# A chunked recurrence on one core: the products and small inverses are made two tiles ahead, and U is solved by two 64-token blocks

## The chip, the core and the metric

The kernel runs on one core of a Trainium2 chip. The metric is the device time of one execution in microseconds (us). The core has five engines: TensorE (PE; its weight loads are shown apart as PEld), VectorE (DVE), ScalarE (ACT), GpSimd (POOL) and the queue that issues transfers (SP). All five run their own instruction streams and wait for each other on semaphores.

## The reference, cut to what matters

One layer of a hybrid encoder block over 1024 tokens and 1024 columns: a norm, one input projection, an RWKV-7 time-mixing group (8 heads of 64) beside windowed attention (8 heads), an output projection, and a SwiGLU feed-forward part. The change is in the recurrence of the RWKV group alone:

```python
def step(S, inp):
    r_t, w_t, k_t, v_t, kk_t, a_t = inp
    sa = jnp.einsum('bhvk,bhk->bhv', S, -kk_t)
    S = (S * w_t[:, :, None, :]
         + sa[..., None] * (kk_t * a_t)[:, :, None, :]
         + v_t[..., None] * k_t[:, :, None, :])
    return S, jnp.einsum('bhvk,bhk->bhv', S, r_t)
_, o = lax.scan(step, S0, xs)
```

The decay is w = exp(-0.6065 * sigmoid(...)), so products of decays over tokens are exponentials of cumulative sums.

## The kernel before

The scan is done in 8 tiles of 128 tokens, in float32. Within a tile the state update becomes a triangular system for each head: U = (I - N)^-1 R, where N (strictly triangular, 128x128) holds the products of alpha (the scaled kk) with beta (the scaled kk times a, the array `ab`), and R = alpha S + K V. Then the outputs are O = rho S + (masked k products) V + (masked beta products) U, and the new state is S + kt V + bt U. The names in the code:

- `cumulative` (L1130): the cumulative sums of the log decays, products of `sgt` with a constant matrix. `exponentials` (L1140, on ACT) turns them into `ein`, `einv`, `eex` (128x512 each), and `prepare` (L1154, on DVE) scales alpha, rho, beta and k with them.
- `against` (L1273): the products of beta ("b", four banks b0 to b3) or k ("k") with rho and alpha, for one of two groups g of heads; `masked` on DVE (L1482) copies their triangles into `NB` (b) and `KB` (k).
- The inverse of (I - N): SP writes NB to DRAM and reads it back so that each of the 64 diagonal 16x16 blocks lies in a lane (`gather`, into `LA`), DVE inverts these (`lanes`, L1532 to L1552, result `LV`), and SP writes `LV` out and reads it back into `XT` (`scatter`), the transposed inverse. PE then doubles the block size: `xa` transposes XT to X (ACT copies it), `t1` = N X (`corners`, DVE masks it into Ts1), `y1` = the update of XT (DVE adds it), `x1` transposes again, `t2`, `y2` likewise for 64x64 blocks, and `x2`, `t3`, `y3` for the last corner, in 64x64 pieces.
- After that come R (ACT copies it to `rs`), the first parts of O, U = XT rs (ACT copies it to `us`), the state S, the rest of O, and for the next tile `following`: its k products and `tokens`, the transposes of beta and k.
- `outputs(t-1)` (job `ot`, L1295) transposes the normalised outputs of the tile before.

Eight PSUM banks are shared by these jobs. Which job gets which bank, and after which other, is the hand-written list `order5`, read by `Plan`: `claim` makes PE wait until the job before it in the bank has been read, `result` makes the reader wait until it is full. Each engine does its instructions in the order in which the code issues them. In the kernel before, the b products of tile t+1 stand inside the block doubling of tile t, in banks 1 and 7, and `lanes(t+1)` stands on DVE right behind the second update of tile t, ahead of `prepare(t+2)`. SP issues, for each tile, the load of `sgt` (after `cum1` of t+1 is full), gather(t+1), scatter(t+1) (its read into XT waits until U of tile t has been made), and the load of `vtk` (the values) once S of tile t is made. In the last tile ACT and DVE also split the mixed outputs into high and low parts (`mix_high`, `mix_low`) for the output projection, which PE starts at L345 after `split_hi` (L304) and `split_lo` (L310) of its first weights.

Of the kernel before, what the change touches and what calls it, by code (L numbers as in the profile page):

```python
# [38 lines left out]
C_ID, C_CUM, C_UP, C_LID, C_LEV, C_BLK, C_ONE, C_PAIR, C_END = np.cumsum([0, P, 2 * P, 2 * P, 2 * P, 2 * P, P, P, 4]).tolist()  # L39
# [5 lines left out]
def constants():  # L45
# [6 lines left out]
    c[:, C_CUM:C_CUM + P] = (s <= t).astype(np.float32) - (s < mid)  # L52
    c[:, C_CUM + P:C_CUM + 2 * P] = (s < t).astype(np.float32) - (s < mid)
# [27 lines left out]
def hybrid_block(nc, x_t, par_in, w_in, w0, w_up, a_up, g_up, sinks, w_out, w_gate_up, w_down, norm_final_g,  # L81
# [18 lines left out]
    with root:  # L100
# [132 lines left out]
        Ts1, Ts2, Ts3 = at("Ts1", 104, [P, H, P]), at("Ts2", 108, [P, H, P]), at("Ts3", 203, [P, H, HD])  # L233
        X, XT = at("X", 112, [P, H, P]), at("XT", 116, [P, H, P])
        ein, einv, eex = (at(n, 120 + 2 * i, [P, NP, P]) for i, n in enumerate(("ein", "einv", "eex")))
# [855 lines left out]
        def plan_next(t):  # L1091
            return ([("k0", t, 4), ("k1", t, 6), ("k2", t, 1), ("k3", t, 7)] if t < NT else []) + (
                [("bt", t, 0), ("kt", t, 2)] if t < NT - 1 else [])

        def plan_b(t, g):
            return [(f"b{2 * g}", t, 1), (f"b{2 * g + 1}", t, 7)] if t < NT else []

        order5 = plan_cum(0) + plan_b(0, 0) + plan_b(0, 1) + plan_next(0) + plan_cum(1)
        for t in range(NT):
            order5 += [("xa0", t, 2), ("xa1", t, 3), ("t10", t, 0), ("t11", t, 6)]  # L1100
            order5 += [("ot", t - 1, 7)] if t else []
            order5 += [("y10", t, 4), ("y11", t, 5), ("x10", t, 2), ("x11", t, 3)] + plan_b(t + 1, 0)
            order5 += [("t20", t, 0), ("t21", t, 6)] + plan_b(t + 1, 1)
            order5 += [("y20", t, 4), ("y21", t, 5), ("x2", t, 2)] + plan_cum(t + 2)
            order5 += [("t3", t, 6), ("R", t, 0), ("y3", t, 4), ("O", t, 5), ("U", t, 2)]
            order5 += ([("S", t, 3)] if t < NT - 1 else []) + plan_next(t + 1)
# [6 lines left out]
         s_var, s_rstd, s_on) = (  # L1113
            sem(f"s5_{n}") for n in ("zero", "seen", "mix", "sg", "v", "prep", "fac", "image", "lane", "inv16", "image2",
                                     "xt", "S", "oc", "osq", "var", "rstd", "on"))
# [14 lines left out]
        def cumulative(pe, t):  # L1130
            pe.wait_ge(s_sgt, 16 * t + 16)
            for j in range(2):
                b = C.claim(pe, f"cum{j}", t)
                for p in (2 * j, 2 * j + 1):
                    mm = pe.matmul(b[:, (p % 2) * 2 * P:(p % 2 + 1) * 2 * P], sgt[:, p * P:(p + 1) * P],
                                   cst[:, C_CUM:C_CUM + 2 * P], start=p % 2 == 0, stop=p % 2 == 1,
                                   skip_group_check=True)
                C.done(mm, f"cum{j}", t)

        def exponentials(act, t, *js):  # L1140
            for j in js:
# [3 lines left out]
                v = b[:, :].rearrange("p (a n) -> p a n", a=2)  # L1145
                c = slice(2 * j, 2 * j + 2)
                act.activation(ein[:, c, :], v[:, :, 0:P], ACT.Exp, scale=-DECAY)
                act.activation(einv[:, c, :], v[:, :, 0:P], ACT.Exp, scale=DECAY)
                act.activation(ecs[:, t, c], v[:, :, P - 1], ACT.Exp, scale=-DECAY)
                act.activation(ems[:, t, c], v[:, :, P], ACT.Exp, scale=DECAY)  # L1150
                ins = act.activation(eex[:, c, :], v[:, :, P:2 * P], ACT.Exp, scale=-DECAY)
                C.read(ins, f"cum{j}", t)

        def prepare(dve, t):  # L1154
# [6 lines left out]
            dve.tensor_tensor(to_alpha, kkn[:, :, c], eex[:, :, :], ALU.mult).then_inc(s_prep, 1)  # L1161
            dve.tensor_tensor(to_rho, rT[:, :, c], ein[:, :, :], ALU.mult).then_inc(s_prep, 1)
# [82 lines left out]
        def stage5_tensor(pe):  # L1245
# [53 lines left out]
            def following(t):  # L1299
                for g in range(2):  # L1300
                    against("k", kT, t, g)
                if t < NT - 1:
                    tokens(t)

            for g in range(2):
                against("b", ab, 0, g)
            following(0)
            cumulative(pe, 1)
            low, high = slice(0, HD), slice(HD, P)
            for t in range(NT):  # L1310
# [6 lines left out]
                corners(1, t)  # L1317
                if t:
                    outputs(t - 1)
                updates(1, t)  # L1320
# [10 lines left out]
                b = C.claim(pe, "x2", t)  # L1331
                for h in range(H):
                    if h % 4 == 0:
                        C.emptied(pe, f"y2{h // 4}", t)
                    mm = pe.transpose(b[low, h * HD:(h + 1) * HD], XT[low, h, low], ident[low, low])
                C.done(mm, "x2", t)
                if t + 2 < NT:
                    cumulative(pe, t + 2)

                b = C.claim(pe, "t3", t)  # L1340
                C.emptied(pe, "x2", t)
                for h in range(H):
                    mm = pe.matmul(b[high, h * HD:(h + 1) * HD], NB[t % 2][low, h, 1, high], X[low, h, low],
                                   start=h == 0, stop=h == H - 1, skip_group_check=True)
                C.done(mm, "t3", t)
# [6 lines left out]
                b = C.claim(pe, "R", t)  # L1352
# [679 lines left out]
```

## Time and profile before

| | us |
|---|---|
| median of 3 runs (lowest, highest) | 1504.01 (1501.05, 1507.19) |
| the profiled execution, own time | 1500.05 |
| its span, first to last instruction | 1498.3 |
| the recurrence in it, from the first transpose of XT (386.3) to the first product of the output projection (655.9) | 269.6 |

| engine | busy us | share of the span |
|---|---|---|
| PE | 1408.6 | 94% |
| DVE | 665.3 | 44% |
| ACT | 396.2 | 26% |
| POOL | 44.1 | 3% |

Times within the trace are counted from the first instruction. An instruction on a PE row is half of one float32 product: a group of 8 products is x16. The ends of matmuls are modelled, so the length of a piece of PE work is read from its start to the start of the next piece. The granted TensorE clock over the whole execution is 0.984 of full speed.

### The profile page before, as it was taken

How to read it: one execution, taken by the hardware profiler on the slowest of the kernel's cores; microseconds unless marked ns; L12 is line 12 of the kernel's file. 1: busy time of each engine (PE TensorE's matmuls, PEld its weight loads, DVE VectorE, ACT ScalarE, POOL GpSimd, SP SyncE). 2: the span in 40 equal slices, each digit the busy share in tenths (PEclk: the TensorE clock that was granted, in tenths of full speed). 3: DMA queues.
4: the chain of work that ended last, by engine and by line, in shares of the span. 5: the costliest groups of instructions: out<-in, count | busy, mean ns of one | idle time of the engine just before them, and what ended most of it. 6: DMA issues, size and time to landing. Idle time of an engine off the chain costs nothing.

```text
span 1498.3 us, 19102 instructions
## 1 busy us (share of the span) xinstructions
PE 1408.6 (94%) x7505; PEld 1167.2 (78%) x7505; DVE 665.3 (44%) x1011; ACT 396.2 (26%) x741; POOL 44.1 (3%) x57
## 2 busy tenths in 40 slices
PE   7999999787699899899999999999999999999994
PEld 6888887565688788788888888888888887888784
DVE  6635312886566666554443332334322333323333
ACT  6010224665123322233232210112101211112113
POOL 0000000212000000000000000000000000000000
PEclk9999999999899999999999999999999999999997
DMA  5111122001112211231111112111111111211112
GB/s 216 43 42 63 64 100 71 1 1 38 39 49 54 68 46 40 96 113 57 44 42 56 38 42 59 57 42 43 41 56 57 42 45 35 61 55 42 35 49 112
DMA packets 57133, 84.49 MB, mean 56 GB/s; under 512 B 19952, under 2 KB 36336, under 8 KB 56816
## 3 DMA queue, kind: packets, MB, share of 16 engines
q1 hardware_dynamic: 57072, 83.64, 17.7%
q8 instruction: 43, 0.70, 0.2%
q14 instruction: 18, 0.15, 0.0%
HBM read 69.44 MB, written 13.64 MB: 55 GB/s over the span
## 4 chain that ended last, share of the span: by engine, by line
PE 82%; DVE 6%; DMA 5%; ACT 4%; issue 1%; ACTq 0%; SPq 0%; DVEq 0%
PE bank L331 62%; PE bank L1248 4%; PE bank L345 3%; PE bank L1278 2%; PE bank L436 2%; ACT scores L970 2%; DMA XT<-inv_scratch 1%; DMA n_scratch<-NB 1%; DMA LA<-n_scratch 1%; PE bank L1255 1%; DVE scores L1002 1%; DMA inv_scratch<-LV 1%; PE bank L870 1%; PE bank L882 1%; PE bank L1370 1%
## 5 line engine op out<-in xcount | busy, mean ns | idle before, releaser
L310 DVE TENSOR_TENSOR ring_wlo<-ring_raw,ring_whi 128x1024 fp32r<-128x1024 f32 (+2 forms) x102 | 114.3, 1121 | 508.6 <-ACT ring_whi L304 508.6
L331 PE MATMUL bank<-x1hi,ring_whi 128*128 128x512 f32 x688 | 267.9, 389 | 0.2 <-DVE ring_wlo L310 0.2
L331 PE MATMUL bank<-x1hi,ring_wlo 128*128 128x512 f32 x688 | 267.7, 389 | 0.0
L331 PE MATMUL bank<-x1lo,ring_whi 128*128 128x512 f32 x688 | 267.6, 389 | 0.0
L304 ACT ACTIVATE ring_whi<-ring_raw 128x1024 fp32r<-128x1024 f32 (+2 forms) x102 | 99.1, 972 | 525.6 <-PE bank L331 503.3
L331 PEld LDWEIGHTS bank<-x1hi,ring_whi 128*128 128x128 f32 x688 | 129.1, 188 | 27.4 <-issue 0.6
L331 PEld LDWEIGHTS bank<-x1lo,ring_whi 128*128 128x128 f32 x688 | 129.1, 188 | 26.8
L331 PEld LDWEIGHTS bank<-x1hi,ring_wlo 128*128 128x128 f32 x688 | 129.1, 188 | 26.7
L331 PE MATMUL bank<-hidhi,ring_whi 128*128 128x512 f32 x308 | 120.0, 390 | 0.0
L331 PE MATMUL bank<-hidhi,ring_wlo 128*128 128x512 f32 x308 | 119.8, 389 | 0.0
L331 PE MATMUL bank<-hidlo,ring_whi 128*128 128x512 f32 x308 | 119.8, 389 | 0.0
L331 PE MATMUL bank<-hhi,ring_whi 128*128 128x512 f32 x288 | 114.8, 399 | 0.0
L331 PE MATMUL bank<-hhi,ring_wlo 128*128 128x512 f32 x288 | 112.4, 390 | 0.0
L331 PE MATMUL bank<-hlo,ring_whi 128*128 128x512 f32 x288 | 112.3, 390 | 0.0
L331 PEld LDWEIGHTS bank<-hidhi,ring_wlo 128*128 128x128 f32 x308 | 57.8, 188 | 12.2
L331 PEld LDWEIGHTS bank<-hidlo,ring_whi 128*128 128x128 f32 x308 | 57.8, 188 | 12.1
L331 PEld LDWEIGHTS bank<-hidhi,ring_whi 128*128 128x128 f32 x308 | 57.8, 188 | 11.8
L331 PEld LDWEIGHTS bank<-hhi,ring_whi 128*128 128x128 f32 x288 | 54.4, 189 | 12.0 <-issue 1.0
L331 PEld LDWEIGHTS bank<-hlo,ring_whi 128*128 128x128 f32 x288 | 54.4, 189 | 11.9 <-issue 1.0
L331 PEld LDWEIGHTS bank<-hhi,ring_wlo 128*128 128x128 f32 x288 | 54.2, 188 | 11.5
L1790 DVE TENSOR_TENSOR gat<-bank,rsb 128x512 f32<-128x512 f32 x44 | 30.4, 692 | 70.9 <-PE bank L331 62.6
L1759 ACT ACTIVATE sil<-gat 128x512 f32<-128x512 f32 x44 | 27.8, 632 | 109.4 <-DVEq L1792 109.3
(270 smaller groups left out, 2018.1 us busy)
## 6 DMA issues: line engine op xcount, KB each, us to landing
ring_raw<-in_w_gate_up SPq DMA_DIRECT2D x44, 512.0 KB, 3.4
ring_raw<-in_w_in SPq DMA_DIRECT2D x20, 512.0 KB, 3.6
ring_raw<-in_w_down SPq DMA_DIRECT2D x16, 384.0 KB, 3.1
ring_raw<-in_w_down SPq DMA_DIRECT2D x16, 320.0 KB, 2.9
xin<-in_x_t SPq DMA_DIRECT2D x8, 512.0 KB, 8.9
n_scratch<-NB SPq DMA_DIRECT2D x8, 512.0 KB, 3.2
XT<-inv_scratch SPq DMA_DIRECT2D x8, 512.0 KB, 4.1
x<-in_x_t SPq DMA_DIRECT2D x2, 2048.0 KB, 8.1
```

Of the source, the lines that this page charges most:

```text
L304: act.activation(self.ring.hi[:, s, 0:self.kt, :], self.ring.raw[:, s, 0:self.kt, :], ACT.Copy).then_inc(self.ring.hi_ready, 1)
L310: dve.tensor_tensor(self.ring.lo[:, s, 0:self.kt, :], self.ring.raw[:, s, 0:self.kt, :], self.ring.hi[:, s, 0:self.kt, :].bitcast(F32), AL ...
L331: mm = pe.matmul(o[:, :], wpart[:, s, k, :], apart[:, k, c], start=i == 0, stop=i == n - 1)
L345: mm = pe.matmul(bank[2 * s + half][:, :], wpart[:, s, ks[n], :], apart[:, ks[n], c], start=n == 0 and i == 0, stop=n == len(ks) - 1 and i ...
L436: mm = pe.matmul(b[:, :], wpart[:, s, k, :], apart[:, k, c], start=k == 0 and i == 0, stop=k == KD - 1 and i == 2)
L870: pe.transpose(b[:, e * P:(e + 1) * P], sb[t % 2][:, h, 0:P], ident)
L882: mm = pe.matmul(bank[6][HD * e:HD * e + HD, p * P:(p + 1) * P], vst[:, j, (p // 2) * HD:(p // 2 + 1) * HD], pt[:, p % 2, j, e, :], start= ...
L970: act.activation(sb[n % 2][:, h, :], sb[n % 2][:, h, :], ACT.Exp, bias=st8[:, 3, h:h + 1], accum_out=st8[:, 5, h:h + 1]).then_inc(s_pe, 1)
L1248: mm = pe.matmul(b[:, j * P:(j + 1) * P], lhs(4 * g + j), rhs(4 * g + j), start=j == 0, stop=j == 3, skip_group_check=True)
L1278: mm = pe.matmul(b[e][:, i * 2 * P:(i + 1) * 2 * P].rearrange("p (a n) -> p a n", a=2), src[r, 2 * g + i, tok(t)], rho_alpha(t, r, 2 * g + ...
L1759: act.activation(sil[:, c], gat[:, c], ACT.Silu).then_inc(s_sil, 1)
L1790: GU.J.read(dve.tensor_tensor(gat[:, c], b[:, :], rsb2[:, c], ALU.mult), f"0{half}")
```

## The change

Four things, all in the recurrence:

1. The cumulative sums are one product over 129 columns (column n is the sum before token n) where there were two of 128. `ein` has 129 columns, `eex` is its first 128, and one of the three large exponentials is gone.
2. The b products of tile t+2 are made at the end of tile t, in banks 4, 6, 1 and 7, and masked at the end of DVE's tile; those of tile 1 ahead of the loop. On DVE `prepare` stands ahead of `lanes`, the masks of k0 and k1 ahead of S, those of k2 and k3 behind O. SP's code is the same, but what its gather waits for comes earlier.
3. `x2`, `t3` and `y3` are left out. U is solved by halves: U_low = XT_low R_low, then N_corner U_low is added into the high half of R, then U_high = XT_high R_high. ACT makes four copies of 64 partitions for it.
4. `outputs(t-1)` stands behind `updates(1)`; `cumulative(t+2)` stands behind the x1 transposes; one group of k products stands between U_high and the beta part of S.

```diff
@@ constants, tiles
-    c[:, C_CUM:C_CUM + P] = (s <= t).astype(np.float32) - (s < mid)
-    c[:, C_CUM + P:C_CUM + 2 * P] = (s < t).astype(np.float32) - (s < mid)
+    c[:, C_CUM:C_CUM + P + 1] = (s < np.arange(P + 1)[None, :]).astype(np.float32) - (s < mid)
...
-            order5 += [("xa0", t, 2), ("xa1", t, 3), ("t10", t, 0), ("t11", t, 6)]
+            order5 += [("xa0", t, 2), ("xa1", t, 5), ("t10", t, 0), ("t11", t, 6), ("y10", t, 4), ("y11", t, 5)]
...
@@ stage5_tensor, the loop over tiles
                 corners(1, t)
+                updates(1, t)
                 if t:
                     outputs(t - 1)
-                updates(1, t)
                 for g in range(2):
                     C.emptied(pe, f"y1{g}", t)
                     transposed("x1", g, t)
-                if more:
-                    against("b", ab, t + 1, 0)
-                corners(2, t)
-                if more:
-                    against("b", ab, t + 1, 1)
-                updates(2, t)
...
                 if t + 2 < NT:
                     cumulative(pe, t + 2)
+                corners(2, t)
+                updates(2, t)
...
+                bu = C.claim(pe, "U", t)
+                for g in range(2):
+                    C.emptied(pe, f"y2{g}", t)
+                pe.wait_ge(s_rlow, t + 1)
+                for h in range(H):
+                    mm = pe.matmul(bu[low, h * HD:(h + 1) * HD], XT[low, h, low], rs_[low, h * HD:(h + 1) * HD],
+                                   start=h == 0, stop=h == H - 1, skip_group_check=True)
+                mm.then_inc(s_u, 1)
                 for p in range(NP):
                     pe.matmul(bo[:, p * P:(p + 1) * P], rho(t, p), S[:, p, :], start=False, stop=False,
                               skip_group_check=True)
...
+                pe.wait_ge(s_ulow, t + 1)
                 for h in range(H):
-                    mm = pe.matmul(b[:, h * HD:(h + 1) * HD], XT[:, h, :], rs_[:, h * HD:(h + 1) * HD],
-                                   start=h == 0, stop=h == H - 1, skip_group_check=True)
-                C.done(mm, "U", t)
+                    mm = pe.matmul(br[high, h * HD:(h + 1) * HD], NB[t % 2][low, h, 1, high],
+                                   us_[low, h * HD:(h + 1) * HD], start=False, stop=h == H - 1, skip_group_check=True)
+                C.done(mm, "R", t)
...
+                C.emptied(pe, "R", t)
+                for h in range(H):
+                    mm = pe.matmul(bu[high, h * HD:(h + 1) * HD], XT[high, h, high], rs_[high, h * HD:(h + 1) * HD],
+                                   start=h == 0, stop=h == H - 1, skip_group_check=True)
+                C.done(mm, "U", t)
+                if more:
+                    against("k", kT, t + 1, 0)
@@ stage5_scalar
+                act.wait_ge(s_r, t + 1)
+                act.activation(rs_[low, :], bank[0][low, :], ACT.Copy).then_inc(s_rlow, 1)
+                act.wait_ge(s_u, t + 1)
+                act.activation(us_[low, :], bank[2][low, :], ACT.Copy).then_inc(s_ulow, 1)
+                keep("R", t, rs_[high, :], high)
+                keep("U", t, us_[high, :], high)
                 if last:
                     mix_high(act, 3)
-                keep("U", t, us_[:, :])
@@ stage5_vector
                 if not last:
-                    lanes(t + 1)
                     if t + 2 < NT:
                         prepare(dve, t + 2)
+                    lanes(t + 1)
+                    masked("k", KB, t + 1, 0, 1)
...
                 if not last:
-                    masked("k", KB, t + 1, 0, 1, 2, 3)
+                    masked("k", KB, t + 1, 2, 3)
                 dve.wait_ge(s_osq, t + 1)
                 dve.tensor_reduce(var, osq[:, :, :], AX_X, ALU.add).then_inc(s_var, 1)
+                if t + 2 < NT:
+                    masked("b", NB[t % 2], t + 2, 0, 1, 2, 3)
```

On PE, from the first corner product of a middle tile to R's first part, the kernel before has these groups (L1248 corners and updates, L1295 `ot`, L1255 `x1`, L1278 the b products, L1335 `x2`, L1135 cumulative, L1343 `t3`, L1354 alpha S):

```order
L1248 MATMUL bank<-X,NB_88 128x128 x8
L1295 MATMUL bank<-cst,on 128x128 x4
L1248 MATMUL bank<-XT,Ts_89 128x128 x8
L1255 MATMUL bank<-cst,XT 128x128 x8
L1278 MATMUL bank<-arv,ab 128x256 x4
L1248 MATMUL bank<-X,NB_88 128x128 x8
L1278 MATMUL bank<-arv,ab 128x256 x4
L1248 MATMUL bank<-XT,Ts_90 128x128 x8
L1335 MATMUL bank<-cst,XT 64x64 x8
L1135 MATMUL bank<-cst,sgt 128x256 x4
L1343 MATMUL bank<-X,NB_88 64x64 x8
L1354 MATMUL bank<-S,arv 128x128 x4
```

At the same place the changed kernel has these:

```order
L1248 MATMUL bank<-X,NB_88 128x128 x8
L1248 MATMUL bank<-XT,Ts_89 128x128 x8
L1295 MATMUL bank<-cst,on 128x128 x4
L1255 MATMUL bank<-cst,XT 128x128 x8
L1136 MATMUL bank<-cst,sgt 128x129 x4
L1248 MATMUL bank<-X,NB_88 128x128 x8
L1248 MATMUL bank<-XT,Ts_90 128x128 x8
L1339 MATMUL bank<-S,arv 128x128 x4
```

The two b groups, `x2` and `t3` are gone from here, `ot` has moved behind the first updates, and the cumulative sums stand ahead of the second corners with 129 columns.

On PE, from R's second part to the products for the next tile, the kernel before has these groups (L1364 `y3`, L1370 and L1373 the first parts of O, L1382 U, L1392 and L1397 S, L1401 the rest of O, L1278 the k products of the next tile):

```order
L1357 MATMUL bank<-vtk,KB 128x64 x8
L1364 MATMUL bank<-XT,Ts_91 64x64 x8
L1370 MATMUL bank<-vtk,KB 128x64 x8
L1373 MATMUL bank<-S,arv 128x128 x4
L1382 MATMUL bank<-rs,XT 128x64 x8
L1392 MATMUL bank<-vtk,kt 128x128 x4
L1397 MATMUL bank<-us,bt 128x128 x4
L1401 MATMUL bank<-us,NB_88 128x64 x8
L1278 MATMUL bank<-arv 128x256 x8
```

The changed kernel has these at that place:

```order
L1348 MATMUL bank<-vtk,KB 128x64 x8
L1356 MATMUL bank<-rs,XT 64x64 x8
L1360 MATMUL bank<-S,arv 128x128 x4
L1364 MATMUL bank<-us,NB_88 64x64 x8
L1374 MATMUL bank<-vtk,kt 128x128 x4
L1377 MATMUL bank<-rs,XT 64x64 x8
L1278 MATMUL bank<-arv 128x256 x4
L1386 MATMUL bank<-us,bt 128x128 x4
L1390 MATMUL bank<-us,NB_88 128x64 x8
L1288 MATMUL bank<-cst,ab 128x128 x4
L1288 MATMUL bank<-cst,arv 128x128 x4
L1278 MATMUL bank<-arv,ab 128x256 x8
```

`y3` is gone, U has become three groups with other work between them (L1356 U_low, L1364 the corner, L1377 U_high), half of the k products has moved up, and all b products (of the tile after the next) stand at the end.

On DVE, from the scaling of a tile to the end of its part for the recurrence, the kernel before has these rows right behind `lanes` (L1159 to L1165 `prepare`, L1611 the state, L1618 to L1627 mean and variance, L1482 the masks):

```order
L1159 TENSOR_TENSOR ab<-ab,einv 128x4x128
L1161 TENSOR_TENSOR arv<-arv,eex 128x4x128
L1162 TENSOR_TENSOR arv<-arv,ein 128x4x128
L1163 TENSOR_TENSOR arv<-arv,einv 128x4x128
L1165 TENSOR_TENSOR facs<-ecs,ems 128x4
L1611 TENSOR_TENSOR Sn<-bank,S 64x4x64 x2
L1618 TENSOR_REDUCE sm<-bank 128x8
L1619 TENSOR_SCALAR sm<-sm 128x8
L1620 TENSOR_TENSOR oc<-bank,sm 128x512
L1482 COPY_PREDICATED KB<-cst,bank 128x2x256 x4
L1627 TENSOR_REDUCE sm<-osq 128x8
```

In the changed kernel `prepare` stands ahead of `lanes`, whose last row is L1534 here:

```order
L1534 TENSOR_REDUCE LV<-LM 64x8x8
L1464 COPY_PREDICATED KB<-cst,bank 128x2x256 x2
L1592 TENSOR_TENSOR Sn<-bank,S 64x4x64 x2
L1599 TENSOR_REDUCE sm<-bank 128x8
L1600 TENSOR_SCALAR sm<-sm 128x8
L1601 TENSOR_TENSOR oc<-bank,sm 128x512
L1464 COPY_PREDICATED KB<-cst,bank 128x2x256 x2
L1608 TENSOR_REDUCE sm<-osq 128x8
L1464 COPY_PREDICATED NB_88<-cst,bank 128x2x256 x4
L1478 TENSOR_TENSOR Ts_89<-bank,cst 128x16x16 x2
```

Two k masks now stand ahead of the state, and four b masks stand ahead of the first corners (L1478) of the next tile.

## Rows read from the trace of the kernel before

**Rows 1.** The waits, 370 to 650 us: who waited for whom, total us, times, longest.

```profile
PE bank L1255 <- DMA XT<-inv_scratch: 22.5, 5, 15.1
PE bank L1295 <- DVE on L1559: 8.5, 7, 1.2
...
PE bank L1343 <- ACT X L1445: 1.5, 2, 0.8
```

**Rows 2.** Engines by stretch, PE PEld DVE ACT POOL busy us, granted clock, DMA share, GB/s.

```profile
386.30:419.90 33.60, 32.53 (x264) 29.14 (x265) 18.58 (x42) 10.34 (x26) 0.00 (x0) 0.94 0.19 52
...
454.50:488.70 34.20, 31.52 (x268) 28.05 (x268) 21.57 (x48) 10.16 (x26) 1.85 (x2) 1.00 0.19 42
...
592.00:627.20 35.20, 28.63 (x253) 25.80 (x253) 20.58 (x45) 7.16 (x14) 2.40 (x4) 0.98 0.18 49
627.20:655.00 27.80, 24.76 (x200) 22.91 (x201) 10.23 (x16) 10.64 (x15) 1.27 (x1) 0.91 0.32 115
```

**Rows 3.** The timeline of PE in tile 2: start us, us, instruction, [idle before, releaser].

```profile
465.79 1.13 PE L1278 MATMUL bank<-arv,ab 64*128 64x256 f32 x8
...
468.86 0.39 PE L1335 MATMUL bank<-cst,XT 64*64 64x64 f32 x4
...
469.76 1.99 PE L1135 MATMUL bank<-cst,sgt 128*128 128x256 f32 x8
...
471.69 1.14 PE L1343 MATMUL bank<-X,NB 64*64 64x64 f32 x16
...
472.76 1.16 PE L1354 MATMUL bank<-S,arv 128*128 128x128 f32 x8
...
475.58 1.14 PE L1364 MATMUL bank<-XT,Ts 64*64 64x64 f32 x16
...
476.65 2.00 PE L1370 MATMUL bank<-vtk,KB 128*128 128x64 f32 x16
...
479.43 1.90 PE L1382 MATMUL bank<-rs,XT 128*128 128x64 f32 x16
...
481.17 1.11 PE L1392 MATMUL bank<-vtk,kt 128*128 128x128 f32 x8
...
482.11 1.06 PE L1397 MATMUL bank<-us,bt 128*128 128x128 f32 x8
...
488.71 1.09 PE L1255 MATMUL bank<-cst,XT 128*128 128x128 f32 x8 [0.85 <-DMA XT<-inv_scratch]
```

**Rows 4.** The timeline of the other engines in tile 2.

```profile
475.38 0.16 DVE L1532 TENSOR_TENSOR LM<-LA 64x8 f32<-64x8 f32 x1 [6.01 <-DMA LA<-n_scratch]
...
481.37 0.60 ACT L1421 ACTIVATE us<-bank 128x512 f32<-128x512 f32 x1 [3.09 <-PE bank L1382]
...
481.83 0.67 DVE L1159 TENSOR_TENSOR ab<-ab,einv 128x512 f32<-128x512 f32 x1
481.93 0.58 SPq L1197 DMA_DIRECT2D inv_scratch<-LV  x1
...
487.07 2.58 DVE L1482 COPY_PREDICATED KB<-cst,bank 128x512 f32<-128x512 uint32 x4 [0.26 <-DVE oc L1620]
```

**Rows 5.** The timeline ahead of tile 0: the last attention copy, the second pair of masks.

```profile
361.61 0.60 ACT L979 ACTIVATE mix<-bank 128x512 f32<-128x512 f32 x1 [0.77 <-PE bank L882]
...
365.60 1.33 DVE L1482 COPY_PREDICATED NB<-cst,bank 128x512 f32<-128x512 uint32 x2 [1.40 <-PE bank L1278]
```

**Rows 6.** The timeline of the last tile: its first transposes, and its end.

```profile
627.20 1.97 PE L1255 MATMUL bank<-cst,XT 128*128 128x128 f32 x8 [3.92 <-DMA XT<-inv_scratch]
...
648.90 1.04 ACT L1169 ACTIVATE mhi<-mix 128x1024 fp32r<-128x1024 f32 x1
...
653.02 0.60 ACT L1421 ACTIVATE us<-bank 128x512 f32<-128x512 f32 x1 [3.07 <-PE bank L1382]
...
654.59 1.23 DVE L310 TENSOR_TENSOR ring_wlo<-ring_raw,ring_whi 128x1024 fp32r<-128x1024 f32 x1 [3.39 <-ACT ring_whi L304]
...
655.87 0.50 PE L345 MATMUL bank<-mhi,ring_whi 128*128 128x512 f32 x1 [0.21 <-DVE ring_wlo L310]
```

More of the change, by code:

```diff
@@ L232, in hybrid_block @@
         NB = [at("NB0", 96, [P, H, 2, P]), at("NB1", 128, [P, H, 2, P])]
[L233 removed]
+        Ts1, Ts2 = at("Ts1", 104, [P, H, P]), at("Ts2", 108, [P, H, P])
         X, XT = at("X", 112, [P, H, P]), at("XT", 116, [P, H, P])
[L235 removed]
+        ein, einv = at("ein", 120, [P, NP, P + 1]), at("einv", 123, [P, NP, P])
         bt, kt_, rs_, us_ = (at(n, kb, [P, W]) for n, kb in (("bt", 126), ("kt", 136), ("rs", 138), ("us", 140)))
@@ L1299, in following @@
             def following(t):
-                for g in range(2):
-                    against("k", kT, t, g)
                 if t < NT - 1:
                     tokens(t)
+                against("k", kT, t, 1)
+                if t + 1 < NT:
+                    for g in range(2):
+                        against("b", ab, t + 1, g)
             for g in range(2):
                 against("b", ab, 0, g)
+            cumulative(pe, 1)
+            against("k", kT, 0, 0)
             following(0)
-            cumulative(pe, 1)
             low, high = slice(0, HD), slice(HD, P)
@@ L1351, in stage5_tensor @@
                     C.emptied(pe, f"k{g}", t)
[L1352 removed]
+                br = C.claim(pe, "R", t)
                 for p in range(NP):
[L1354 removed]
+                    pe.matmul(br[:, p * P:(p + 1) * P], alpha(t, p), S[:, p, :], start=p == 0, stop=False,
                               skip_group_check=True)
                 for h in range(H):
[L1357 to L1366 removed]
+                    mm = pe.matmul(br[:, h * HD:(h + 1) * HD], KB[:, h, 1, :], vtk[:, h * HD:(h + 1) * HD],
+                                   start=False, stop=False, skip_group_check=True)
+                mm.then_inc(s_r, 1)
                 bo = C.claim(pe, "O", t)
@@ L1371, in stage5_tensor @@
                               stop=False, skip_group_check=True)
+                bu = C.claim(pe, "U", t)
+                for g in range(2):
+                    C.emptied(pe, f"y2{g}", t)
[4 more added lines that the diff above has]
+                mm.then_inc(s_u, 1)
                 for p in range(NP):
@@ L1574, in stage5_vector @@
             dve.wait_ge(s_z5, 6)
-            masked("k", KB, 0, 0, 1, 2, 3)
+            masked("k", KB, 0, 0, 1)
+            prepare(dve, 1)
             lanes(0)
-            prepare(dve, 1)
+            masked("k", KB, 0, 2, 3)
             dve.wait_ge(s_z5, 8)
+            masked("b", NB[1], 1, 0, 1, 2, 3)
             for t in range(NT):
@@ L1586, in stage5_vector @@
                     outputs(t - 1)
-                if not last:
-                    masked("b", NB[(t + 1) % 2], t + 1, 0, 1)
-                else:
+                if last:
                     mix_low(dve, 0)
                 corners(2, t)
-                if not last:
-                    masked("b", NB[(t + 1) % 2], t + 1, 2, 3)
-                else:
+                if last:
                     mix_low(dve, 1)
```

88 lines of the change are left out of this document (25 added, 63 removed).

## The prediction

> **What bounds the kernel now.** I read the waits first, then the engines by stretch, then one tile on the timeline. TensorE is the engine to watch. In a middle tile it is busy 31.5 of 34.2 us at the full granted clock [rows 2], and ScalarE and VectorE are busy 10 and 22 us. So the recurrence is a chain on PE with three gaps. The first is the arrival of the inverted blocks in XT: 22.5 us over 5 tiles, 15.1 of it ahead of tile 0 [rows 1], 0.85 at the end of tile 2 [rows 3] and 3.92 ahead of tile 7 [rows 6]. The second is `ot`, which waits for DVE's `on` in seven tiles, 8.5 us in all, 1.2 each [rows 1]. The third is 0.8 us for ACT ahead of `t3` where no cumulative sums lie between (tiles 6 and 7) [rows 1]. All else in a tile is PE work end to end, so removed PE work counts in full as long as nothing new ends later.
>
> **A middle tile, step by step.** It takes 34.2 us now [rows 2].
>
> (a) `x2`, `t3`, `y3` and U fall away. By starts on PE: `x2` 469.76 - 468.86 = 0.90, `t3` 472.76 - 471.69 = 1.07, `y3` 476.65 - 475.58 = 1.07, U 481.17 - 479.43 = 1.74 [rows 3]; together 4.78. What comes are three groups of eight 64x64 products on 64 columns, the form of `t3`: 3 x 1.07 = 3.21. Net -1.57.
>
> (b) The cumulative sums take 471.69 - 469.76 = 1.93 with 256 columns [rows 3]. No row has 129 columns. Below lies half, 0.97 (the S part, eight instructions of 128 columns, takes 482.11 - 481.17 = 0.94); above lies no gain at all, should an odd number of columns or the odd start of the second half in the bank cost something. I take half, since the time goes with columns in every row here: -0.95, with 0 as the other end.
>
> (c) `ot` behind the first updates: `on` is made on DVE right after the first masks as before, while PE does 2 us of updates. Its wait of 1.2 goes, and a little comes back as the updates no longer overlap with it: -1.0.
>
> (d) XT. In the new order DVE does `prepare` (2.5 us: 481.83 to the Sn pair) and then `lanes`, 481.83 - 475.38 = 6.45 us [rows 4], from the end of the second updates. With my tile those end 12.8 us after the tile's first transpose, so LV is ready at 12.8 + 2.6 + 6.5 = 21.9. In the trace XT is there 488.71 - 481.93 = 6.8 us after the issue of LV's write [rows 3, 4], which makes 28.8. The gather in front is out of the way: its NB is masked by 2 us into the tile, and the two transfers that took from 468.9 to 475.3 have until 15.4. The other condition, that XT is overwritten only when U is done, is met from 22.1, before the write has landed (24.5). PE is back at its transposes at about 30.3. XT is 1.5 us early, and the wait of 0.85 is gone.
>
> (e) The new tail. The second b group needs banks 1 and 7, so the masks of k2 and k3, and DVE can begin these only when the second k group is done, 2.2 us after O. Two masks take 2.58 / 2 = 1.3 [rows 4]; PE has the first b group of 1.07 to do meanwhile. +0.4.
>
> (f) The hand-overs of U. Each of the four copies of 64 partitions is priced as `us`: PE's next group began at 481.17 and the copy ended 481.97, then PE went on at 482.11 [rows 3, 4], so 0.8 to 0.9 must be covered. Cover is: 1.8 (O's first part) for R_low, 0.94 (rho S) for U_low, 0.94 (kt V) for R_high, 1.0 (the k group) for U_high. I take 0; with a cover gone it is 0.85 each. This is the thinnest place: three covers exceed the need by 0.1.
>
> (g) The b masks (2.6 us) now stand on DVE ahead of the next tile's first corner. They end 2.2 us into it; the corner's product ends at 2.5. 0, by 0.3 us of room. What is queued behind them are Ts1, `on` and the first updates.
>
> (h) ACT: one exponential of three less, four short copies for five longer ones; nothing on the path.
>
> Sum: 34.2 - 1.57 - 0.95 - 1.0 - 0.85 + 0.4 = 30.3 (30.2 to 30.5).
>
> A rule to weigh here: the Trainium skill, TensorEngine Tiling (Array Packing), Key Properties, says that a change of tiling mode drains the engine. I count twelve changes in a middle tile before (both b groups, `x2`, `t3`, `y3`, k) and nine after. The trace shows no gap at such a change: `t3` and `y3`, with one on either side, take 1.07 for 16 instructions each, and what follows starts at once [rows 3]. Should each cost the 0.1 that an end lies behind the next start, the change would gain 0.3 more a tile, 2 us in all; the sum leaves it out.
>
> **All tiles.** Tiles 1 to 5 last 592.0 - 419.9 = 172.1 us [rows 2] and would take 5 x 30.4 = 152: -20. Tile 0 has no `ot` and no wait at its end: a, b and e, -2.1. Tile 6 (35.2 us): a -1.6, c -1.0, the wait ahead of `t3` -0.8, no b products any more (two groups of 1.07 [rows 3]) -2.1, and the wait for XT of 3.9: `lanes` comes directly behind the updates there, XT is bounded by U_high plus 4.3 us, and behind U_high PE has both k groups, bt U and the rest of O, 4.7 us. Together -9.4.
>
> Tile 7 (627.2 to 655.87, 28.7 us): its clock was granted at 0.91 in the mean and its transposes took 1.97 where they take 1.09 at the full clock [rows 2, 6], after the wait. With that wait gone I take back 0.09 x 27.8 = 2.5. Then a -1.6, c -1.0, `t3`'s wait -0.8. Against it: R_high is not covered there, +0.85; and `mix_high` now stands between U's copy and the split of the first output weights, 1.04 more [rows 6] before L310 (1.23) and L345, of which about 1 shows: +1.5 together with DVE's share. -3.5.
>
> Ahead of tile 0: the second pair of NB masks waited 1.40 us for PE, since both b groups used banks 1 and 7 [rows 5]. Now they follow at once, but bank 6 is held by the attention copy until 362.2 [rows 5], which moves the first pair by 0.6. -0.8, and XT comes that much earlier.
>
> Total: -0.8 - 2.1 - 20 - 9.4 - 3.5 = -35.8. The profiled execution took 1500.05 us, 1.75 more than its span, and would take 1464.3. It lies 4 us under the median of the runs shown, 1504.01; on that basis I get 1468 and take 1469, since a sum of removed gaps rather leaves small ones out.
>
> **The rivals.**
>
> 1. The hand-overs show. For: the need of 0.85 is as large as the cover. Against: at 482.11 PE did go on without a gap behind a cover of 0.94. If the three thin ones cost 0.3 each, +0.9 x 7 = 6, 1475; if they are not covered at all, 3 x 0.85 x 7 = 18, 1487. Chance 0.12, likeliest near 1476.
>
> 2. DVE becomes the chain. Its order is now corners, updates, `prepare`, `lanes`, masks, state, mean, masks, b masks; its 22 busy us fit in 30.4 with the waits for PE between. If masks at the head or `lanes` come late by 1 to 2 us in each tile, XT or the first corners do too: 7 to 12 us, 1476 to 1481. Against: the room of 1.5 at XT. Chance 0.13.
>
> 3. Cumulative sums on 129 columns cost as much as before: 0.95 x 7 = +6.7, 1476. Nothing in the trace speaks for it but that no such row exists. Chance 0.06.
>
> 4. More comes back than summed (a change of mode costs something, tile 0's clock recovers since PE has b products during its wait): 2 to 7 us, 1462 to 1467. Inside the forecast's own range for the most part; beyond it 0.05.
>
> 5. The other side. `lanes(t+1)` stands on DVE ahead of the masks of k, the state and the mean. If LA lands late, all of these wait, and with them the b masks that release the next gather: a loop. It decides from LA landing 15.4 us into the tile; then every further us is paid in every tile, and to eat 36 us it must be late by 5 us more. In the trace the two transfers take 6 to 9 us and start at 2. Chance 0.02, 1510.
>
> The forecast itself, hand-overs covered and XT early, has 0.62 and its own range is 1463 to 1474.
>
> **The numbers.** 0.5% is 7.5 us, about what a measurement of this kernel can tell from no change. Only rival 5 and a far case of rival 1 end within it or beyond: faster 0.95, same 0.03, slower 0.02. For 8 in 10 the range takes the forecast's own and the near parts of rivals 1 to 3: 1461 to 1480.
>
> **What the profile after should show.** Tiles 1 to 5 at 30.2 to 30.6 us from transpose to transpose, with PE never waiting for XT but ahead of tile 0 (some 14 us still). Cumulative sums 1.0 us a tile. `ot` without a wait. U's three groups 1.07 each and gaps below 0.1 in front of them. A gap of 0.3 to 0.5 between the two b groups. Tile 6 at 26 us, and tile 7 at the full granted clock, with some 1.5 us of waiting for `ring_wlo` ahead of its end. The prediction is wrong if XT, the b masks or ACT's short copies appear among PE's waits with more than 0.5 us a tile, or if the granted clock falls inside tiles 1 to 6.

## The result, and the profile after

The changed kernel takes 1457.72 us in the median (1457.51 to 1458.26, 4 runs) against 1502.53 (1500.26 to 1507.19, 4 runs): a ratio of 0.970 (0.968 to 0.973). Run again beside other kernels on another chip it gave 0.972 (0.969 to 0.974). That is 42 to 45 us, where 35 were forecast, and 3 us below the range. The profiled execution of it took 1458.26 us, with a span of 1456.5 against 1498.3 [rows 1 to 6 are of the latter], 41.8 us less. All but 0.2 us of that lies in the recurrence. By the starts of the first transposes of each tile and of the first product of the output projection, in the two traces:

| piece | before | after | change | forecast |
|---|---|---|---|---|
| start to tile 0 | 386.28 | 385.50 | -0.8 | -0.8 |
| tile 0 | 33.6 | 30.7 | -2.9 | -2.1 |
| tiles 1 to 5 | 172.1 | 146.8 (29.35 each) | -25.3 | -20 |
| tile 6 | 35.2 | 25.4 | -9.8 | -9.4 |
| tile 7 | 28.7 | 25.1 | -3.6 | -3.5 |
| all behind it | 842.4 | 843.1 | +0.6 | 0 |

One middle tile on PE's timeline (start us, us, instruction, [idle before, releaser]) answers to [rows 3]:

```profile
445.55 1.09 PE L1255 MATMUL bank<-cst,XT 128*128 128x128 f32 x8
446.98 2.02 PE L1248 MATMUL bank<-X,NB 128*128 128x128 f32 x16 [0.34 <-ACT X L1410]
448.84 1.95 PE L1248 MATMUL bank<-XT,Ts 128*128 128x128 f32 x16
450.63 0.60 PE L1295 MATMUL bank<-cst,on 128*128 128x128 f32 x4
451.07 1.04 PE L1255 MATMUL bank<-cst,XT 128*128 128x128 f32 x8
451.94 1.06 PE L1136 MATMUL bank<-cst,sgt 128*128 128x129 f32 x8
452.83 1.95 PE L1248 MATMUL bank<-X,NB 128*128 128x128 f32 x16
454.62 1.95 PE L1248 MATMUL bank<-XT,Ts 128*128 128x128 f32 x16
456.41 1.06 PE L1339 MATMUL bank<-S,arv 128*128 128x128 f32 x8
...
461.98 1.16 PE L1360 MATMUL bank<-S,arv 128*128 128x128 f32 x8
463.07 1.14 PE L1364 MATMUL bank<-us,NB 64*64 64x64 f32 x16
464.14 1.16 PE L1374 MATMUL bank<-vtk,kt 128*128 128x128 f32 x8
465.23 1.14 PE L1377 MATMUL bank<-rs,XT 64*64 64x64 f32 x16
466.30 1.13 PE L1278 MATMUL bank<-arv 64*128 64x256 f32 x8
...
470.10 0.61 PE L1288 MATMUL bank<-cst,ab 128*128 128x128 f32 x4
...
471.07 1.14 PE L1278 MATMUL bank<-arv 64*128 64x256 f32 x8
472.04 1.03 PE L1278 MATMUL bank<-arv,ab 64*128 64x256 f32 x8
473.84 1.14 PE L1278 MATMUL bank<-arv,ab 64*128 64x256 f32 x8 [0.77 <-DVE KB L1464]
474.90 1.09 PE L1255 MATMUL bank<-cst,XT 128*128 128x128 f32 x8
```

The only idle times of some size left are 0.34 for ACT's first copy of X and 0.77 between the two b groups. `ot` and the x1 transposes follow without a wait, and each of the three groups of U takes 1.07 to the start of the next group.

The same tile on the other engines (answers to [rows 4]): the end of `lanes`, the write of LV, the read into XT.

```profile
465.26 0.68 DVE L1534 TENSOR_REDUCE LV<-LM 64x64 f32<-64x512 f32 x1
465.96 0.58 SPq L1197 DMA_DIRECT2D inv_scratch<-LV  x1
466.41 0.59 ACT L1410 ACTIVATE us<-bank 64x512 f32<-64x512 f32 x1 [1.57 <-PE bank L1377]
...
474.18 2.57 DVE L1464 COPY_PREDICATED NB<-cst,bank 128x512 f32<-128x512 uint32 x4
```

The write of LV is issued 20.4 us into the tile (the forecast had 21.9). By the 6.8 us of [rows 3, 4], which is an estimate here, XT is there at 472.8, 2.1 us before PE wants it. The copy of U_high takes 0.59 us for 64 partitions, and `us` took 0.60 for 128 [rows 4].

By stretch (columns as in [rows 2]), tile 0 without its last 0.4 us, and a middle tile:

```profile
385.50:415.80 30.30, 29.45 (x254) 27.36 (x256) 17.68 (x41) 9.12 (x23) 0.00 (x0) 0.93 0.21 57
445.50:474.90 29.40, 28.29 (x262) 26.14 (x261) 21.86 (x49) 8.90 (x23) 1.90 (x3) 1.00 0.22 59
```

PE is busy 28.3 of 29.4 us, where it was 31.5 of 34.2 [rows 2]. So of the 4.8 us between these two tiles 3.2 are busy time of PE and 1.6 are idle time.

### The profile page after: what moved, and what is told of

It reads as the page before. It is cut to its first block, busy times and chain, and to the rows that moved or that the text cites. A ratio compares the mean times of both kernels' runs of the same rounds, so it can differ in the third digit from the quotient of the medians.

```text
span 1456.5 us, 18955 instructions
## 1 busy us (share of the span) xinstructions
PE 1385.0 (95%) x7441; PEld 1151.8 (79%) x7441; DVE 665.3 (46%) x1011; ACT 386.1 (27%) x717; POOL 43.9 (3%) x57
## 4 chain that ended last, share of the span: by engine, by line
PE 68%; DVE 2%; ACT 2%; issue 1%; DMA 1%; ACTq 0%; DVEq 0%; SPq 0%
PE bank L330 51%; PE bank L1248 4%; PE bank L344 3%; PE bank L1278 1%; PE bank L1348 1%; PE bank L1342 1%; PE bank L1390 1%; PE bank L1255 1%; PE bank L1360 1%; PE bank L1377 1%; PE bank L1364 1%; PE bank L1356 1%; PE bank L1386 1%; PE bank L1374 1%; PE bank L1339 0%
## 5 line engine op out<-in xcount | busy, mean ns | idle before, releaser
L1773 DVE TENSOR_TENSOR gat<-bank,rsb 128x512 f32<-128x512 f32 x44 | 30.4, 692 | 70.9 <-PE bank L330 62.6
```

What stands on the lines that cost most here:

```text
L1773: GU.J.read(dve.tensor_tensor(gat[:, c], b[:, :], rsb2[:, c], ALU.mult), f"0{half}")
```

## The experiments

Ratios are to the kernel before on the same chip. The question that the result left was why more came back than was summed. I also wanted to know which part of the change does it.

**1. `ot` put back ahead of the first updates, in the changed kernel.**

```diff
                 corners(1, t)
-                updates(1, t)
                 if t:
                     outputs(t - 1)
+                updates(1, t)
```

> The changed kernel with one edit undone: the transposes of the outputs (ot) stand ahead of the first updates again. Theory A (the place of ot was worth 1.9 us a tile: its own wait of 1.2, the wait of 0.5 of the x1 transposes that it now fills, and an end of 0.2): a middle tile goes from 29.35 to 31.2 us, the whole to 7 x 1.9 = 13 us more than the changed kernel, about 0.979 of before. Theory B (the prediction's step: 1.0 us a tile): a middle tile of 30.3, 7 us more, about 0.975.

Measured: 1470.53 us, 0.979 (0.977 to 0.982), and middle tiles of 31.05. That is close to theory A: 1.7 us a tile, where A had 1.9 and B 1.0.

**2. That edit alone in the kernel before.**

> The kernel before with that one edit alone: ot behind the first updates. It lies ahead of the masks of the b products that start the gather, so the transfers move up with it. Theory A: 1.9 us a tile in tiles 1 to 7, 13 us in all, 0.991 of before. Theory B: 1.0 us a tile, 7 us, 0.995.

Measured: 1487.67 us, 0.991 (0.989 to 0.994), 15 us by the medians; theory A again. Tiles 1 to 5 take 32.6 us in the mean, 1.8 less than before. One of them, PE's timeline:

```profile
485.51 2.02 PE L1248 MATMUL bank<-X,NB 128*128 128x128 f32 x16 [0.34 <-ACT X L1421]
...
490.63 1.13 PE L1278 MATMUL bank<-arv,ab 64*128 64x256 f32 x8
491.69 2.05 PE L1248 MATMUL bank<-X,NB 128*128 128x128 f32 x16
493.67 1.13 PE L1278 MATMUL bank<-arv,ab 64*128 64x256 f32 x8
...
516.58 1.06 PE L1255 MATMUL bank<-cst,XT 128*128 128x128 f32 x8 [0.83 <-ACT kt L1421]
```

Two things are to be seen. The second corners, between two b groups, take 493.67 - 491.69 = 1.98 us, and the same 16 instructions take 454.62 - 452.83 = 1.79 in the changed kernel, where they stand among full-size products. And the first transposes wait 0.83 us for ACT's copy of kt, since both use bank 2: behind the wait for XT there was a second one, about as long as the 0.85 of [rows 3]. The trace of before has it too, with 0.83 at the ends of tiles 0, 4 and 5, and the rows of the prediction do not show it.

**3. The cumulative sums over 129 columns, alone in the kernel before** (the edits of `constants`, `cumulative`, `exponentials` and `prepare` of the change, nothing else).

> The kernel before with the cumulative sums over 129 columns alone. Theory A (the cuts add up; PE work counts in full wherever it is): 7 x 1.0 = 7 us faster, 0.995. Theory C (in the old order the sums lie behind the start of the gather, so the arrival of XT, 20.2 us after that start, takes back what PE gains): the wait for XT ahead of a tile grows by about 1 us, from 0.85 to 1.9, and the time stays within 1.5 us of before, 0.999 to 1.000.

Measured: 1502.93 us, 1.001 (0.999 to 1.003). By the time that is theory C. The profiled execution is one of the longer ones (1508.00, of 1498.01 to 1508.78). Its tiles 1 to 4 take 34.3 us in the mean, where they took 34.5, though each has 1 us less of PE work. Two of its first transposes:

```profile
453.42 1.07 PE L1253 MATMUL bank<-cst,XT 128*128 128x128 f32 x8 [1.51 <-DMA XT<-inv_scratch]
...
521.96 1.07 PE L1253 MATMUL bank<-cst,XT 128*128 128x128 f32 x8 [2.00 <-ACT kt L1419]
```

Not all that was gained went to these waits. In tile 6 of this execution, behind a wait of 3.75 us, the granted clock is 0.72, and the tile takes 41.4 us for 35.2.

**4. U by halves, alone in the kernel before** (`x2`, `t3`, `y3` removed, the three groups of U, ACT's four copies, one k group ahead of the state).

> The kernel before with U solved by halves alone (x2, t3 and y3 left out, half of the k products between U_high and the state). Theory A: 1.6 us a tile, 11 to 13 us in all, 0.992. Theory C (all of it lies behind the start of the gather): within 2 us of before, with the wait for XT ahead of a tile grown to about 2.5 us; 0.999.

Measured: 1503.30 us, 1.001 (0.999 to 1.003). Theory C, and more than that: the trace (1505.56 us) shows a lower granted clock behind the longer waits.

```profile
453.41 1.50 PE L1255 MATMUL bank<-cst,XT 128*128 128x128 f32 x8 [2.17 <-DMA XT<-inv_scratch]
...
523.74 1.97 PE L1255 MATMUL bank<-cst,XT 128*128 128x128 f32 x8 [3.57 <-DMA XT<-inv_scratch]
...
384.50:632.50 248.00, 219.74 (x1801) 195.81 (x1801) 147.78 (x321) 65.08 (x163) 11.40 (x14) 0.94 0.18 48
```

Behind a wait of 3.57 us the transposes take 1.97, as at the lower of the two levels (1.2 GHz), and behind one of 2.17 they take 1.50; the granted clock over tiles 0 to 6 is 0.94, where a window over the same tiles of the kernel before shows 0.99. So there a tile has fewer products and takes longer, up to 37 us.

**5. All parts but the b products ahead** (3 and 4 and the place of `ot` together, in the kernel before).

> The kernel before with all parts of the change but one: cumulative sums over 129 columns, U by halves, ot behind the first updates; the b products stay one tile ahead, inside the block doubling, with lanes ahead of prepare. Theory C (work behind the start of the gather is hidden behind the transfers for XT, so only ot's 12 us count): about 0.991 of before, as ot alone gave, or worse where the longer wait lowers the granted clock. Theory A (the parts add up): 31 us faster, 0.979.

Measured: 1495.95 us, 0.996 (0.995 to 0.998): less than `ot` alone gave. Adding two cuts of PE work to experiment 2 made it slower; the two ran on different chips, but the intervals of their ratios lie apart. Waits of 2.7 to 4.9 us stand ahead of the transposes of tiles 1 to 7, and in six of these the lower level shows behind the wait, in the transposes (1.8 to 2.0) or in the corners that follow. Only behind the shortest wait, the second row, do both run at the full clock:

```profile
457.19 1.94 PE L1253 MATMUL bank<-cst,XT 128*128 128x128 f32 x8 [4.91 <-ACT kt L1410]
...
491.80 1.09 PE L1253 MATMUL bank<-cst,XT 128*128 128x128 f32 x8 [2.66 <-DMA XT<-inv_scratch]
```

**6. The b products ahead, alone** (the new banks, DVE's new order, one k group ahead of the state, in the kernel before).

> The kernel before with the other part alone: b products two tiles ahead, the new order of banks and of DVE, half of the k products ahead of the state; 256 columns, U from the whole inverse with x2, t3 and y3, and ot ahead of the updates stay. PE does the same work less the waits for XT and for kt's bank: a middle tile of about 33.2 us, 1 us less; tile 6 loses its b products (2.1) and 3.9 of waiting, tile 7 the lower clock (2.5): 5 x 1 + 6 + 2.5 + 1 = 14 us, 0.990. With the one before: 14 + 13 = 27 of the 45 us that the whole gives, so that some 18 us belong to the two together.

Measured: 1521.04 us, 1.013 (1.009 to 1.017). Slower, and my expectation wrong. The timeline of the profiled execution, the longest of the six (1531.95):

```profile
485.25 0.69 DVE L1162 TENSOR_TENSOR ab<-ab,einv 128x512 f32<-128x512 f32 x1 [9.02 <-ACT eex L1154]
...
496.27 0.66 PE L1291 MATMUL bank<-cst,arv 128*128 128x128 f32 x4 [2.80 <-DVE Sn L1614]
```

`prepare` now stands ahead of `lanes` on DVE, and with ACT's second exponential still behind the copies for R and `y3`, DVE stands idle 9 us. All behind it is late, up to the state, whose bank PE needs for the transposes of kt.

**7. As 6, with cumulative sums and exponentials early, as in the change.**

```diff
                     transposed("x1", g, t)
+                if t + 2 < NT:
+                    cumulative(pe, t + 2)
                 corners(2, t)
...
                     mix_high(act, 1)
+                if t + 2 < NT:
+                    exponentials(act, t + 2, 0, 1)
```

> As the b products ahead alone, but with the cumulative sums of t+2 behind the x1 transposes and both exponentials behind ACT's copies of X, as in the changed kernel. In the run before, DVE waited 9.0 us a tile for the last exponential ahead of prepare, so lanes, the k masks and the state came late and PE waited 2.8 us a tile for Sn ahead of the transposes of kt. Theory: that was the whole of the loss; with the exponentials early DVE's order costs nothing and the estimate of the run before holds, 14 us faster than before, 0.990 (0.987 to 0.993). Rival: the new order of DVE costs time by itself (b masks ahead of the corners, masks ahead of the state): no faster than before, 1.00.

Measured: 1493.82 us in the median, ratio 0.998 (0.995 to 1.002). DVE's wait is gone and no tile but the first waits for XT, so the cause of 6 stands. But the 14 us did not come: 6 by the medians, and 3 by the ratio. The 12 runs spread from 1490.7 to 1516.0 us, and the four longest, above 1508, have the four lowest granted clocks (0.970 to 0.976, the others 0.986 to 0.988). In the profiled one (1491.09) a middle tile takes 34.34 us, no less than before; most of what this execution gained lies in tile 6, 29.2 us for 35.2. The middle tile:

```profile
452.89 1.09 PE L1258 MATMUL bank<-cst,XT 128*128 128x128 f32 x8
...
468.14 1.11 PE L1345 MATMUL bank<-X,NB 64*64 64x64 f32 x16 [0.77 <-ACT X L1451]
...
487.23 1.09 PE L1258 MATMUL bank<-cst,XT 128*128 128x128 f32 x8
```

What XT's wait gave up went to a new wait ahead of `t3`, whose cover the cumulative sums had been (0.77), and to the one between the b groups (0.77). The step from this tile to the changed kernel's 29.35 is PE work and `ot`, piece by piece: `ot` 1.70 (from the first corners to the end of x1, 6.66 to 4.96), the sums 0.84, U with its corner work and the wait ahead of `t3` 2.45; together 4.99. Experiments 1 and 8 show the first two by themselves. The 2.45 of U is what is left, and no run undoes the halves alone in the changed kernel.

**8. The cumulative sums over 256 columns again, in the changed kernel** (127 of the columns are computed and not read).

> The changed kernel with the product of the cumulative sums streaming 256 columns again, of which ACT reads the first 129 as before (the other 127 are products with the next columns of the constants and are not used). In the kernel before, cutting these columns gave nothing. Theory (in the new order all PE work counts): 1.0 us a tile and 7 to 8 us in all slower than the changed kernel, 0.975 to 0.976 of before. Rival (they are hidden here too, since ACT's copy of X must be done before the second corners): less than 2 us.

Measured: 1461.90 us, 0.975 (0.972 to 0.977), against 0.970 to 0.972: some 5 us. From the start of the sums to the next group it is 1.73 where it was 0.89, in six tiles, 5.0 us. The 7 to 8 us expected counted 1.0 a tile.

```profile
454.59 1.89 PE L1136 MATMUL bank<-cst,sgt 128*128 128x256 f32 x8
456.32 1.95 PE L1248 MATMUL bank<-X,NB 128*128 128x128 f32 x16
```

The same cut was worth nothing in the kernel before (experiment 3) and its full length here.

**9. The cover of one hand-over taken away** (the kt part of the state moved ahead of the corner product, so that nothing covers the copy of R_high).

> The changed kernel with the products of kt and the values moved ahead of the corner product, so that nothing lies between the corner product, the copy of R_high and U_high. If a hand-over needs 0.8 to 0.9 us and the cover hides it (the prediction's step f), PE now stalls for about 0.7 us a tile in front of U_high, as it does in the last tile of the changed kernel (0.68), less 0.1 to 0.2 for two changes between full and quarter tiles that fall away: 7 tiles, 3 to 5 us more than the changed kernel. If the hand-overs would have been free anyway, no difference.

Measured: 1467.07 us, 0.975 (0.973 to 0.977), 6 to 8 us over the changed kernel by the ratios, where 3 to 5 were expected. A middle tile takes 29.91, +0.56 as expected, but in three of the seven tiles 1.6 us come on top: tiles 3 and 5 take 31.5, and tile 6 takes 27.56 where the changed kernel has 25.39.

```profile
446.25:476.16 29.91, 28.12 (x263) 26.07 (x261) 21.80 (x48) 8.90 (x23) 1.85 (x3) 1.00 0.22 58
476.16:507.67 31.51, 29.72 (x262) 27.35 (x260) 21.92 (x48) 8.90 (x23) 1.83 (x3) 0.95 0.22 56
...
496.40 1.14 PE L1377 MATMUL bank<-rs,XT 64*64 64x64 f32 x16 [0.68 <-ACT rs L1410]
...
499.01 2.08 PE L1386 MATMUL bank<-us,bt 128*128 128x128 f32 x8
...
590.11 2.07 PE L1278 MATMUL bank<-ar,arv 64*128 64x256 f32 x8
```

In the second the groups from 1.1 us behind the start of U_high on ran at the lower level (2.08 where 1.16 is usual), and the granted clock is 0.95. The last row shows the same in tile 6, where 1.13 is usual. The stall of 0.68 is there in both kinds of tile; why the clock fell in some and not in the others is open.

**10. A version to beat both: both k groups ahead of the state's beta part, all k masks ahead of the state.**

```diff
                 if more:
-                    against("k", kT, t + 1, 0)
+                    for g in range(2):
+                        against("k", kT, t + 1, g)
...
-                    masked("k", KB, t + 1, 0, 1)
+                    masked("k", KB, t + 1, 0, 1, 2, 3)
```

> The changed kernel with both groups of k products between U_high and the beta part of the state, and all four k masks on DVE ahead of the state. In the changed kernel PE waits 0.77 us in each of six tiles between the two groups of b products for the masks of k2 and k3, which stand behind the mean. Theory: that wait goes, nothing new is late (the b masks on DVE end as the first corners are due): 0.6 to 0.8 us a tile, 4 to 5 us faster than the changed kernel, 0.967 of before. Rival: the four masks push the state, the mean and the b masks back on DVE, and the first corners of the next tile wait for them: no gain or up to 3 us slower.

Measured: 1454.08 us, 0.967 (0.965 to 0.970): 4 to 6 us less than the changed kernel by the ratios, about as expected, though the intervals of the two overlap; between the traces, from the first transpose to the output projection, it is 4.7. The b groups now stand in one piece and a tile takes 28.3 us, 1.0 less:

```profile
469.47 2.00 PE L1278 MATMUL bank<-arv,ab 64*128 64x256 f32 x16
...
583.99 0.66 PE L1255 MATMUL bank<-cst,XT 128*128 128x128 f32 x4 [1.28 <-DVE oc L1602]
```

Part of the rival came true as well, as the second row shows. Nothing stands between O and the first transposes of the last tile now, DVE has four masks to do before it reads O, and the transposes, which use the bank of O, wait 1.28 us for that. That tile takes 1.1 us longer.

**11. The same, with the fourth `mix_high` ahead of the copy of U_high in the last tile.**

> As the one before, and in the last tile the high part of the fourth mixed row is made ahead of the copy of U_high again instead of behind it: the wait for ring_wlo at the end of the recurrence (1.06 us in the changed kernel) falls to about 0, so 1 us less again, 5 to 6 us faster than the changed kernel.

Measured: 1452.82 us, 0.966 (0.964 to 0.968). That this edit gives its 1 us is not shown. There was no wait left for it to remove: in the trace of experiment 10 the last part of O, 1.8 us at the full clock, took 3.5 at the lower level with no wait for `ring_wlo` behind it. Here it takes 608.09 - 604.66 = 3.4. In the changed kernel it had been 2.4 and a wait of 1.06, also 3.5.

```profile
604.66 3.68 PE L1391 MATMUL bank<-us,NB 128*128 128x64 f32 x16 [0.68 <-ACT us L1411]
...
608.09 0.77 PE L344 MATMUL bank<-mhi,ring_whi 128*128 128x512 f32 x1
```

## Why the prediction was off

The mechanism was right: XT stopped being the bound, and the removed PE work counted. The sum was too small by 6 us against the profiled execution, 5.3 of them in tiles 1 to 5, where a tile takes 29.35 us and 30.3 to 30.4 were forecast. The other 5 of the 11 us between 1469 and 1457.7 are the basis. The prediction added 4 us because the profiled execution of before lay that far below the median, and 1 more for small gaps left out. The runs of the changed kernel lie within 0.8 us of each other, the profiled one is the longest of them, and nothing had to be added.

Piece by piece, from the starts on PE in the tile at 454.46 before (34.25 us) and the one at 445.55 after (29.35):

| piece of a middle tile | summed | measured |
|---|---|---|
| (a) U by halves, with the groups around it | -1.57 | -1.43 |
| (b) cumulative sums | -0.95 | -1.04 |
| (c) `ot` | -1.0 | -1.89 |
| (d) the waits at the tile's end | -0.85 | -0.97 |
| (e) the stall between the b groups | +0.4 | +0.73 |
| second corners and updates | 0 | -0.41 |
| k group, beta part of S, rest of O | 0 | +0.11 |
| together | -3.97 | -4.90 |

**Step (c), `ot`, is the step that failed.** It was sized at -1.0 with "a little comes back". In the kernel before, a middle tile had these rows:

```profile
455.89 2.02 PE L1248 MATMUL bank<-X,NB 128*128 128x128 f32 x16 [0.34 <-ACT X L1421]
459.12 0.63 PE L1295 MATMUL bank<-cst,on 128*128 128x128 f32 x4 [1.21 <-DVE on L1559]
...
461.37 1.34 PE L1255 MATMUL bank<-cst,XT 128*128 128x128 f32 x8
462.74 1.13 PE L1278 MATMUL bank<-arv,ab 64*128 64x256 f32 x8
```

From the start of the first corners to the end of x1 the piece took 462.74 - 455.89 = 6.85 us and takes 451.94 - 446.98 = 4.96 now: -1.9, and experiments 1 and 2 give 1.7 and 1.8 by the tile. Nothing comes back. `ot` no longer waits 1.2, and standing behind the updates it fills the time in which the second half of x1 waited for DVE's update of XT: x1 took 1.37 and takes 0.87. That was an idle time which I had left in the tile. The step is short by 0.9 a tile, 0.89 of the 0.93 that the sum of a middle tile lacks.

**Step (a)**, -1.57, measured -1.4: 4.78 and 3.21 were right to 0.01, but rho S and kt V, now between the 64x64 groups of U, take 1.09 each and took 0.94, and R gets 0.2 shorter.

**Step (b)**: 1.93 to 0.89, -1.04, for -0.95. Eight instructions of 129 columns take 0.89 us here, at the odd place in the bank too, and the eight of alpha S with 128 take as much (456.41 to 457.30). Rival 3 fell.

**Step (d)**: from the start of the transposes of beta and kt to the next group it was 1.94 (486.77 to the 488.71 of [rows 3]) and is 471.07 - 470.10 = 0.97, -0.97 for -0.85.

```profile
486.77 0.66 PE L1288 MATMUL bank<-cst,ab 128*128 128x128 f32 x4
```

What was not seen is that the copy of kt in bank 2 made PE wait about as long as XT did; the change moves it to bank 3. In tile 0, where XT did not, the prediction had "no wait at its end", and tile 0 gained 0.8 more than forecast.

**Step (e)**: the stall between the b groups was 0.73 by the starts and 0.77 in the trace's own count, for +0.4: DVE began the masks of k2 and k3 0.3 us after their product, and PE had only 1.03 us of other work.

**Step (f)**: right, with more room than it had counted on. The thin covers take 1.07 to 1.09 here, where 0.94 to 1.0 were forecast, and they hide a hand-over of 0.8 to 0.9; PE's longest wait there is below 0.1. With one cover gone it is 0.68 (experiment 9). Rival 1 fell.

**Step (g) and rival 2**: right, the b masks delay nothing. Rival 2 is a real mechanism all the same: experiment 6 is DVE's in-order queue as the bound, late through `prepare` and not through LA as rival 5 had it, and slower than before by 1.3%. The change avoids it by moving the sums and the exponentials up, a part that I had priced at nothing and without which the rest does not pay (experiments 6 and 7).

**Rival 4** named what came, more comes back than summed: the 6 us are inside its 2 to 7. It had 0.05 beyond the forecast's own range. Of its two causes the changes of mode gave about 1 us, and the clock of tile 0 did not recover: 0.93 is granted where it was 0.94. Most of what came back was `ot`, which it did not name.

**The changes of tiling mode.** The sum left them out, as I read no gap behind `t3` and `y3` [rows 3]. But these have a change on each side, so their 1.07 held it already. Groups of the same form in both surroundings show it: 1.98 against 1.79 for 16 instructions with a change on both sides, 0.1 us for each. The second corners and updates, freed of the b groups, gave 0.4 a tile and R 0.2; the neighbours of U's groups took 0.4 to 0.5 back. The net is some 0.2 a tile, 1 us or a little more in all, where the prediction put 0.3 and 2 us beside its sum.

The Trainium skill, TensorEngine Tiling (Array Packing), Key Properties, says that a change of tiling mode drains the engine. These longer groups agree with it; that draining is what the 0.1 us is spent on is not shown by itself.

**Tiles 6 and 7** came out at the forecast sums (-9.8 and -3.6 for -9.4 and -3.5), but partly by luck. Without cumulative sums to do, PE waits 0.34 us there for ACT's copy of X ahead of the second corners, so x1 with that wait takes 1.38 as before and `ot` gives only 1.4 in tile 6; experiment 1 loses 1.4 in that tile too. In tile 7 the granted clock is 0.96 and not the full one that was forecast, the first transposes with the wait behind them take 2.16 where a middle tile has 1.43, since they wait for DVE's read of O, and the wait for `ring_wlo` is 1.06 for 1.5. The start (-0.8) came as forecast.

What the experiments add is which part earns what. Alone in the kernel before, the sums give nothing, the halves nothing, `ot` 13 to 15 us, the b products ahead lose 19 as first made and gain at most some 6 with early sums; all but the b products gain 5. Together it is 42 to 45. The move of the b products takes no work off PE in a middle tile, but with it the gather of the next tile is issued 2.0 us into a tile (447.55 - 445.55) instead of 14.1 (468.56 - 454.46), and only then are the other cuts time:

```profile
468.56 0.37 SPq L1185 DMA_DIRECT2D n_scratch<-NB  x1
```

The same instruction in the changed kernel:

```profile
447.55 0.37 SPq L1185 DMA_DIRECT2D n_scratch<-NB  x1
```

For the sums this is shown both ways, by experiments 3 and 8. For the halves it is shown in the old order (experiment 4), and in the new one only by what is left of the sum in experiment 7.

## What to carry to other kernels

Ask of each cut of work on the busiest engine whether it lies ahead of or behind the start of the transfer that the engine waits for next: behind it, it only lengthens the wait. Where the waits had grown to 1.7 to 4.9 us here, the granted clock fell behind most of them, and with two more cuts the kernel took longer than with one (experiments 5 and 2). When a transposed or moved group is priced, count the waits on both sides of its new place, since it may fill one that no row calls by its name. And when instructions are put ahead of others in an in-order queue, look up first when their own inputs come.

## What the runs showed of the hardware that was not expected

A stall of 0.68 us in a stretch of float32 products whose other idle times are 0.34 and 0.77 us was followed by the lower clock in three of seven tiles, and cost 1.6 us each time (experiment 9). In the changed kernel, which has the other two idle times and not this one, tiles 1 to 6 ran at a granted clock of 1.00. The kernels that wait for a transfer at every tile head spread widely from run to run: the kernel before had 1494.5 to 1508.0 us over 17 runs on one chip, the changed kernel on the same chip 1457.3 to 1460.3 over 5. That this comes from the length of the transfers and what it does to the clock would fit experiments 4 and 5, but no run shows it by itself.
